# First layer of a hybrid trunk: rotation, local attention and decays in one stage

## The reference, cut to what matters

```python
def gla_log_decay(a_low, wa2, ba):
    return jax.nn.log_sigmoid((a_low @ wa2 + ba).astype(jnp.float32)) / GLA_TAU
...
    cum = jnp.cumsum(ac, axis=2)      # inside a chunk
...
def even_mixer(ul, uc, w_in, wa2, ba, norm_g, sink, w_out, ang, need_ctx):
    ...
    o_c, s_f, s_b = gla_bidir(cq, ck, cv, claf, clab, zero, zero)
    o_l, _, _ = gla_bidir(lq, lk, lv, llaf, llab, s_f, s_b)
    a_l = swa_latent(apply_rope(lsq, ang), apply_rope(lsk, ang), lsv, csk, csv, sink)
    y_l = jnp.concatenate([gla_output(o_l, lg, norm_g), a_l], axis=-1) @ w_out
```

## Time and profile before

| | us |
|---|---|
| median of three runs (lowest, highest) | 2827.79 (2823.54, 2829.77) |
| profiled execution, its own time | 2822.94 |
| its span, first to last instruction | 2821.2 |

### The profile page before, as it was taken

One profiled execution on the slowest core, in us unless ns is written; L12 is line 12 of the kernel. 1 busy time (PEld: TensorE's weight loads), 2 busy tenths in 40 slices (PEclk: granted clock), 3 DMA queues, 4 the chain that ended last, 5 costly groups with the idle time before them and its releaser, 6 DMA issues. The chain is left out here.

```text
span 2821.2 us, 30247 instructions
## 1 busy us (share of the span) xinstructions
PE 2472.2 (88%) x8861; PEld 1128.8 (40%) x8862; DVE 1188.8 (42%) x2415; ACT 422.9 (15%) x891; POOL 856.4 (30%) x1012
## 2 busy tenths in 40 slices
PE   6999794596599999999997897998399999999996
PEld 2565352442333333333333543554233333333332
DVE  2998255733632323333339312322543232323327
ACT  2000144211000000000003311332000000000002
POOL 0111102101245454545423001001154545454532
PEclk9999896798799999999998899999699999999997
DMA  7756000210599999999967300100579989989857
GB/s 252 231 188 235 19 1 1 66 67 33 208 360 365 365 349 350 364 364 353 366 254 289 97 30 9 60 22 31 202 291 344 342 329 335 339 335 333 336 202 276
DMA packets 163887, 634.29 MB, mean 225 GB/s; under 512 B 51711, under 2 KB 58283, under 8 KB 113507
## 3 DMA queue, kind: packets, MB, share of 16 engines
q10 hardware_dynamic: 59984, 389.57, 37.1%
q0 software_dynamic: 55280, 129.67, 12.6%
q1 hardware_dynamic: 48548, 114.13, 10.9%
HBM read 609.96 MB, written 74.58 MB: 243 GB/s over the span
## 5 line engine op out<-in xcount | busy, mean ns | idle before, releaser
L1759 POOL DMA_INDIRECT xg<-rows_x,p_idx x520 | 529.3, 1018 | 231.9 <-issue 120.9
L1847 PE MATMUL p_gu<-ring,p_xT 128*128 128x512 f32 x1024 | 454.2, 597 | 26.1 <-DVE p_xT L2088 26.1
L1859 PE MATMUL p_gu<-ring,p_xT 128*64 x1024 | 453.2, 595 | 0.0
L1860 PE MATMUL p_gu<-ring,p_xT 128*64 128x512 f32 x1024 | 453.2, 595 | 0.0
L2094 DVE TENSOR_TENSOR p_hid<-p_gu,p_sg 128x256 f32<-128x256 f32 x128 | 54.4, 425 | 579.0 <-ACT p_sg L1972 579.0
L1847 PEld LDWEIGHTS p_gu<-ring,p_xT 128*128 128x128 f32 x1024 | 191.7, 192 | 243.0 <-issue 243.0
L2088 DVE STREAM_TRANSPOSE p_xT<-xg 128x1024 f32<-128x1024 f32 x130 | 263.6, 2028 | 28.7 <-DMA xg<-rows_x,p_idx 26.9
L2104 DVE COPY p_ys<-p_y 128x512 f32<-128x512 f32 x128 | 88.5, 691 | 367.5 <-PE p_y L1888 189.5
L1859 PEld LDWEIGHTS p_gu<-ring,p_xT 128*64 128x64 f32 x1024 | 135.0, 137 | 263.8 <-issue 256.1
L1886 PE MATMUL p_y<-ring,p_hT 128*64 x512 | 235.1, 602 | 5.1 <-issue 5.1
L1875 PE MATMUL p_y<-ring,p_hT 128*128 128x512 f32 x512 | 236.9, 606 | 0.0
(11 more groups left out here) (445 smaller groups left out, 2975.9 us busy)
## 6 DMA issues: line engine op xcount, KB each, us to landing
ring<-in_w_exp_gate ACTq DMA_DIRECT2D x120, 1024.0 KB, 7.3
ring<-in_w_exp_up ACTq DMA_DIRECT2D x120, 1024.0 KB, 10.3
ring<-in_w_exp_down ACTq DMA_DIRECT2D x120, 1024.0 KB, 7.8
ring<-rows_y SPq DMA_DIRECT2D x80, 512.0 KB, 12.7
p_wm<-in_w_mod POOLq DMA_DIRECT2D x24, 1024.0 KB, 6.8
cat_e<-in_w_mod POOLq DMA_DIRECT2D x16, 1024.0 KB, 6.1
xg<-rows_x,p_idx POOLq DMA_INDIRECT x520, 5.3
p_wmod<-in_w_mod SPq DMA_DIRECT2D x4, 2048.0 KB, 15.7
```

Of the source, the lines that this page charges most:

```text
L1759: nc.gpsimd.indirect_dma_start(out=xg[q][:, part * D // QUADS:(part + 1) * D // QUADS], out_offset=None, in_=tr.rows_x[:, :].rearrange("t ...
L1847: mm = nc.tensor.matmul(gu[q][:], xT[q][:, k, :], w[:, :, k, :], start=(k == 0), stop=(k == KD - 1))
L1859: nc.tensor.matmul(gu[q][lower, :], xT[q][:, k, lower], wa[:, :, k, :], start=first, stop=last)
L1860: mm = nc.tensor.matmul(gu[q][upper, :], xT[q][:, k, upper], wb[:, :, k, :], start=first, stop=last)
```

## The change

`rotate` (which the second layer still uses), `window_attention` and `gla_decays` become one stage, `local_attention`, for the first layer. Its stream has, in order on each engine:

- SP: mask and sinks, then the rotation's tables, then, when DVE has cleared `wa`, the decays' four small loads.
- PE: the scores of tile 0, the six swaps, the logits of the four parts (now in the two buffers `raw`, so that part 2 waits for DVE's and ACT's reading of part 0, and part 3 for that of part 1), and then the tiles' steps as before. The first scores of tile 1 wait for the reading of parts 2 and 3, those of tile 2 for the rotation.
- DVE: clears, masks of tile 0, the rotation with the sine product of part n+1 ahead of the sum of part n, the four splits, and then the steps with the decays' operations between them (`decays_between`).
- ACT: Exp of tile 0, the absolute values, and then per tile as before; Exp and Ln of the four parts (`log_decays`) behind the copy of tile 0's result; the two Exp of parts 0 and 1 behind that of tile 3, of parts 2 and 3 behind that of tile 4.
- POOL: the cosines, the keys' products. Its four clears of `qb` and `sm` move to `gla_states`.

Two stage boundaries fall away. Tiles of the decays share the memory of others: `qa` and `kb` that of `even_project`'s buffers `wm`, the rotation's tables and `wa` that of `cat`, `reset` that of the last block of `pT`, the swaps' PSUM banks those of `turn`, `ot` and `op`.

```diff
-def window_attention(tr, sqT, skT, sv, cat):
+def local_attention(tr, sqT, skT, sv, cat, qkT, aT, qa, kb, carry):
...
+                sp.dma_start(swap[:], dr["c_swap"]).then_inc(rope_loaded, 16)
+                sp.dma_start(rope, dr["c_rope"]).then_inc(rope_loaded, 16)
+                sp.wait_ge(cleared, 1)
+                for d in range(2):
+                    sp.dma_start(wa[d * GRANK:(d + 1) * GRANK, d, :], dr["gla_wa2"][0, d]).then_inc(wa_loaded, 16)
+                    sp.dma_start(ba[:, 2 * d:2 * d + 2], dr["gla_ba"][0, d].rearrange("(j p) -> p j", p=P),
+                                 allow_slow_non_contiguous=True) \
+                        .then_inc(wa_loaded, 16)
...
+                    if t == 1 and head < 2:
+                        pe.wait_ge(split, 6 + 2 * head)
+                        pe.wait_ge(absed, 6 + 2 * head)
+                    if t == CT and head == 0:
+                        pe.wait_ge(rotated, len(rotating))
...
+                def swap_halves():
+                    pe.wait_ge(rope_loaded, 32)
+                    for n, x in enumerate(rotating):
+                        if n >= 4:
+                            pe.wait_ge(sines, n - 3)
+                        nc.tensor.matmul(swaps[n % 4], swap[:], x, start=True, stop=True).then_inc(swapped, 1)
+
+                def decay_logits(x):
+                    if x >= 2:
+                        pe.wait_ge(split, 2 * (x - 1))
+                        pe.wait_ge(absed, 2 * (x - 1))
+                    else:
+                        pe.wait_ge(masked, SH - 1 + x)
+                    for hf in range(2):
+                        mm = nc.tensor.matmul(raw[x % 2][:, hf * 512:hf * 512 + HALF],
+                                              wa[:, x // 2, (x % 2) * P:(x % 2 + 1) * P],
+                                              aT[:, hf * HALF:(hf + 1) * HALF], start=True, stop=True)
+                    mm.then_inc(logits, 1)
...
                 for head in range(SH):
                     score(0, head)
+                swap_halves()
+                pe.wait_ge(wa_loaded, 64)
+                for x in range(4):
+                    decay_logits(x)
                 for t in range(NT):
...
+                def decays_between(t, i):
+
+                    if 1 <= t < CT + 1 and i in (2, 5):
+                        sum_decays(2 * (t - 1) + (i == 5))
+                    if t == 3 and i == 1:
+                        turn_round()
+                    if t == 3 and 3 <= i < 7:
+                        centre(i - 3)
+                    if t == 4 and i % 2 == 0 and i < 10:
+                        for d in range(2):
+                            sum_carry(d, i // 2)
+                    if t == 5 and i % 2 == 1 and i < 8:
+                        scale_queries(i // 2)
...
                 maxima(0)
+                turn_halves()
+                for x in range(4):
+                    split_logits(x)
                 for t in range(NT):
                     for i, (head, quad) in enumerate(steps(t)):
...
                         if t and i == BACK:
                             norm(t - 1)
+                        decays_between(t, i)
...
                 exps(0)
+                act.wait_ge(wa_loaded, 64)
+                for x in range(4):
+                    act.wait_ge(logits, x + 1)
+                    for hf in range(2):
+                        nc.scalar.activation(qa[:, x, hf * HALF:(hf + 1) * HALF], raw[x % 2][:, hf * 512:hf * 512 + HALF],
+                                             ACT.Abs, bias=ba[:, x:x + 1]).then_inc(absed, 1)
                 for t in range(NT):
                     place(t)
                     if t + 1 < NT:
                         exps(t + 1)
                     place_o(t)
+                    if t == 0:
+                        log_decays()
+                    if t in (3, 4):
+                        for x in (2 * t - 6, 2 * t - 5):
+                            factors(x)
```

More of the change, by code:

```diff
@@ L385, in even_project @@
         product, read_dve, read_act = ph.sem("product"), ph.sem("read_dve"), ph.sem("read_act")
-        wm = [ph.sb(f"wm{i}", [P, KD, MC])[:] for i in range(MBUF - 2)]
+        wm = [decays[:, i * KD * MC:(i + 1) * KD * MC].rearrange("p (k n) -> p k n", n=MC) for i in range(MBUF - 2)]
         wm += [spare[:, 2 * i:2 * i + 2, :].rearrange("p t (k n) -> p (t k) n", n=MC) for i in range(2)]
@@ L663, in _ @@
                 load_ahead(sp)
+            @block.gpsimd
+            def _(pool):
+                for i in range(2):
+                    other = slice((1 - i) * GDK, (2 - i) * GDK)
+                    nc.gpsimd.memset(qb[other, :, :, i, :], 0.0)
+                    nc.gpsimd.memset(sm[other, :, :, i, :], 0.0)
             @block.tensor
@@ L1085, in place, with log_decays, factors @@
                             nc.scalar.copy(pT[:, b, 4 * q:4 * q + 4, :], turn[1][:]).then_inc(placed_a, 1)
+                def log_decays():
+                    for x in range(4):
+                        act.wait_ge(absed, 2 * x + 2)
+                        nc.scalar.activation(qa[:, x, :], qa[:, x, :], ACT.Exp, scale=-1.0).then_inc(exped, 1)
+                    for x in range(4):
+                        act.wait_ge(exped, x + 1)
+                        nc.scalar.activation(qa[:, x, :], qa[:, x, :], ACT.Ln, bias=tr.ones[:, 0:1]).then_inc(logged, 1)
+                def factors(x):
+                    act.wait_ge(relative, x + 2)
+                    nc.scalar.activation(qa[:, x, :], kb[:, x, :], ACT.Exp, scale=1.0 / GTAU).then_inc(factor_q, 1)
+                    act.wait_ge(factor_q, x + 1)
+                    nc.scalar.activation(kb[:, x, :], kb[:, x, :], ACT.Exp, scale=-1.0 / GTAU).then_inc(factor_k, 1)
                 def place_o(t):
@@ L1098, in _ @@
                     place_o(t)
+                    if t == 0:
[3 more added lines that the diff above has]
+                            factors(x)
+                act.wait_ge(carried, 4 * (NT - 1))
+                for d in range(2):
+                    b = ORDER[d][0]
+                    for lo, hi in ((0, b), (b + 1, NT)):
+                        if lo < hi:
+                            nc.scalar.activation(carry[:, d, lo:hi, :], carry[:, d, lo:hi, :], ACT.Exp, scale=1.0 / GTAU)
 def even_mixer(tr, layer):
@@ L1110, in even_mixer @@
             early, aT = sb("early", [P, 3, NT * GH * GDV]), sb("aT", [2 * GRANK, T])
+            decays, carry = sb("decays", [P, 2 * 4 * T]), sb("carry", [P, 2, NT, 2])
+            qa, kb = (decays[:, i * 4 * T:(i + 1) * 4 * T].rearrange("p (x t) -> p x t", x=4) for i in range(2))
             qkT = early[:, 0, :].rearrange("p (x t) -> p x t", x=4)
```

223 lines of the change are left out of this document (93 added, 130 removed).

## The result

| | before | after |
|---|---|---|
| median of five runs each (lowest, highest), us | 2827.79 (2818.42, 2837.02) | 2799.95 (2796.57, 2805.25) |
| profiled execution, its own time, us | 2822.94 | 2797.42 |
| its span, us | 2821.2 | 2795.4 |

What follows compares the result with a forecast made beforehand. PE, busy 88% of the span, was taken to set the pace. Removing 50.5 us, delays of 18.9 us and a 1.5 us gain in states gave -33.1: 2794.7 us on the median; own range 2789 to 2799, wide range 2784 to 2806.

Steps and rivals of the forecast that it cites:

- rival 1: Tile 1: TensorE's clock falls in PE's wait and stays at 1.2 GHz until the values; +6 us, 2801; chance 0.27.
- the clock does otherwise in tile 1: Sign of failure: TensorE's clock in tile 1 behaves otherwise than forecast, whose sum counted no fall there.
- What is removed: Decays stage and its boundary, from the attention's end to the states stage: 50.5 us go.
- The opening and tile 0: Opening: tile 1's masks begin 2.4 us later; tile 0 left as it is, near the low clock.
- Tile 1: DVE waits 3.35 us for ACT's logarithms, PE stands still 4.2; with a second sum, +5.8 us, between 3.3 and 8.6.
- Tile 2: Two running sums of 2.65 us between steps, each about 1.1 over PE's slack; values 2.0 us late, bounds 0.5 and 5.3.
- Tile 3: Turning round and four centrings on DVE between steps, 5.8 us against slack and idle time: +2.3, between 0.7 and 5.8.
- rival 4: Clock falls in tile 1 and stays low through tiles 1 to 5: +64, so 31 us slower, 2859; chance 0.03.
- Tile 3's idle time: DVE's idle time in tiles 1 to 5, spread over 42 steps: some 0.7 us a step, 2.0 to 2.8 usable.
- Tile 4: DVE's small sums blocked by POOL's products, 3.4 us less 1.5 of slack: +2.2, between 0.3 and 4.0.
- Tile 5: Four Exp ahead of ACT's first quad, 3.35 us, and DVE's last two products, 0.85: +4.2, between 3.3 and 6.
- States stage: POOL's clears hide in idle time; PE arrives at 2.4 GHz: a gain of 1.5 us, between 0 and 2.9.

Runs made afterwards that it cites:

- the run with the clock held: Changed kernel, nothing moved, with idle products of PE (results unused) where it waits in tiles 1, 2, 3 and 5; median 2801.0 us, ratio 0.992.
- the fastest run: Changed kernel with the decays' work moved to idle times, idle products in the opening and every other step of tiles 0 to 4; median 2777.1 us, ratio 0.983.
- the three kernels that had it: Moved-work kernel with a product in every step (2796.1 us) or every other step (2777.1), and the changed kernel, nothing moved, with products in tiles 1 to 5 (2794.4).
- The two kernels that got them: Moved-work kernel with products in the opening, then also every other step (2783.7 to 2777.1 us); changed kernel, nothing moved, given products (2800.0 to 2794.4).

## Why the prediction was right, and where it was not

The sign, the main mechanism (one stage less, its work in the attention stage's idle time, paid back in part by waits) and the range of 2784 to 2806 were right. On the median 2800.0 us came for 2794.7. That lies just outside the forecast's own 2789 to 2799 and nearest to rival 1, at 2801. The prediction had also written that it fails if the clock does otherwise in tile 1, and there the clock did. Its path was wrong in this point, and that the total came within 5.3 us is in part luck: misses of 10.1 us one way and 3.0 the other.

- **What is removed**: 50.5 us, and it was. The clears hid: 10.5 us of POOL beside a states stage that became shorter.
- **The opening and tile 0**: +1.1 us for 2.4. The opening took 2.0 us more, as reckoned to 0.4; tile 0 gave 0.9 back, since the clock rose earlier in its values.
- **Tile 1**: waits of 4.05 and 4.96 us for 3.35 and 4.2. The tile grew by 8.6 for 5.8. This is the step that failed: "TensorE's clock falls in PE's wait in tile 1" was given 0.27, and the sum went without it. The run with idle products takes it apart: with the clock held, the tile takes 18.5, +6.4, so the fall cost 2.2 us (rival 1 had put it at 6).
- **Tile 2**: +4.6 for 2.0; held, +2.0. **Tile 3**: +3.0 for 2.3; held, +1.4. The sum had no falls there, and rival 4, the only one that reached these tiles, had one long low stretch through all of them.
- **Tile 3's idle time**: the prediction divided DVE's idle time in tiles 1 to 5 by 42 steps; these tiles have 52, which makes it 0.5 us a step and not 0.7. The +2.3 had used the lower end of its 2.0 to 2.8, so the term stays.
- **Tile 4**: +0.4 for 2.2. Only one small sum ran into POOL's products. In the run with idle products two did, as the forecast had it.
- **Tile 5**: +8.2 for 4.2, the largest miss. The wait of 3.29 us is the forecast's 3.35, but PE came out of it at the low clock, values included. Held: 16.0, +4.1.
- **States stage**: -2.0 for -1.5, PE arriving at 2.4 GHz. Arriving so isn't enough: in the run with a product in every other step PE arrived at the high clock too, but it fell within 2 us, and the stage took 28.3 us for the change's 26.7. (PE had idled for 36.0 us ahead of this stage before, not for the 33 of the prediction; nothing rests on it.)

So, by the run with the clock held, the terms for the delays of tiles 1, 2, 3 and 5 were right to about 1 us each, and the misses there, 10.1 us together, are those of the clock (10.5 us went in these four tiles when it was held). The opening, tile 0 and tile 4 gave 3.0 back. Rival 1 was right in kind, not in place and price: not one fall of 6 us but falls in four tiles, of 2.2, 2.5, 1.7 and 4.1 us.

That waits cause the falls was my theory, and it fell as a full account. Four runs, the one with the logarithms first, the one with everything behind the last tile, the one with more products in tile 4 and the kernel before itself, have tiles of 30.5 to 31.7 us without a new wait in them. What is shown: the clock falls in stretches of scores of 64 rows and turns and at the start of the values behind them, behind waits from 0.3 to 5 us; a fall early in a tile's steps lasts until its values or into them (but for the one of 3 us in tile 0 of the fastest run), which costs 8.7 to 12 us in tiles 2 and 3; shifts elsewhere in the program move the falls; one idle product of full height in every step or every other step went with a clock of 1.00 from tile 1 on in the three kernels that had it, in the one profiled execution of each. Whether the full height does it, or only that PE has more to do, no run separates. What stays open is why a fall hits one tile and not the next, and how often each kernel is hit: there is one profile for most of them. The change's two agreed, yet its timed executions lie up to 8.5 us apart. Some of the 27.8 us may be falls that the kernel before suffers and the changed one doesn't, or the other way round: against the second execution of before, with its fall, the changed kernel's span is 37.8 us shorter, against the first 25.8.

## What to carry to other kernels

Work woven into another engine's idle time is free only where nobody waits for that engine before it is done: behind the last steps of tiles 3 and 4, while the values run, 10 us of DVE work cost nothing; behind tile 1, whose values are over in 1.94 us, 2.7 us of it cost 1.2; between the steps delays came back as waits of PE. Where TensorE does light work (half-height products, transposes), look at the granted clock stretch by stretch before and after, in more than one execution; a tile that keeps the high clock in one execution may lose it in the next, and the price (8.7 us here) is larger than the delays that one weighs. A few idle products in its stream, at about 0.45 us each and in every other step, can be the cheaper half of the trade. The two kernels that got them came out about 5 us faster (50.3 us under the kernel before for 44.9, and 33.0 for 27.8), though the intervals of the ratios overlap. The changed kernel's timed runs then lay within 3.2 us instead of 8.7, the other's within 12.0 instead of 6.4.

## What was unexpected of the hardware

The granted clock fell from 1.00 to 0.50 in the midst of steps in which PE had gone from one instruction to the next for over 2 us (389.34 to 392 in tile 3 of the kernel before; the tile's 19.56 us of PE work became 28.83). More feeding wasn't always better: with a product in every step tile 0 ran at 0.52, with one in every other step at 0.87, in one profiled execution each. And a change of ACT's function set cost 1.28 us, the next ACTIVATE starting right behind it (367.74 + 1.28, 369.03), without the further drain that the Trainium skill (ScalarE: Activation LUTs, What ACT_TABLE_LOAD costs) adds to it.
